# Moving x_lo by 128 bytes and the shared area by 256 in SBUF, in a one-core kernel of float32r matmuls

## What is computed

```python
proj = x @ w_in                                  # 2048 to 9552 columns
y = mem_cross_attention(x, mem, w_q_mem, w_kv_mem, w_o_mem)
g, u = jnp.split(x @ w_in, 2, axis=-1)           # the feed-forward layer
y = (jax.nn.silu(g) * u) @ w_out
```

## Time and profile before

| | before |
|---|---|
| time, median of 3 runs | 2236.54 us (2236.3 to 2237.06) |
| the profiled execution's span | 2233.7 us |
| TensorE matmul busy | 2221.8 us, 99% |
| TensorE weight load busy | 1840.4 us, 82% |
| VectorE busy | 1299.9 us, 58% |
| ScalarE busy | 1050.6 us, 47% |
| GpSimd busy | 179.5 us, 8% |
| read from HBM | 417.98 MB, 188 GB/s |

### The profile page before, as it was taken

How to read it: one execution, slowest core, us unless ns; L and a number is a source line. 1 busy time by engine, 2 the same in 40 slices (tenths; PEclk the granted TensorE clock), 3 DMA queues, 4 the chain that set the end, 5 groups by cost and what they waited for, 6 DMA issues and landing times.

```text
span 2233.7 us, 29393 instructions
## 1 busy us (share of the span) xinstructions
PE 2221.8 (99%) x10217; PEld 1840.4 (82%) x10217; DVE 1299.9 (58%) x1569; ACT 1050.6 (47%) x1263; POOL 179.5 (8%) x187
## 2 busy tenths in 40 slices
PE   9999999999999999999999999999999999999999
PEld 8888888888888888888888888888888888888887
DVE  5555655666667754454445445566656656645674
ACT  4444445555444644433444344446445444545643
POOL 1000000001304220000000000003000000200020
PEclk9999999999999999999999999999999999999999
DMA  7755654556856466656665566554566655665554
GB/s 234 227 171 163 195 158 144 190 171 216 256 180 214 134 198 190 206 199 194 188 191 187 197 190 187 191 205 151 170 188 194 207 179 183 211 189 174 169 189 165
DMA packets 216871, 421.30 MB, mean 189 GB/s; under 512 B 15400, under 2 KB 19536, under 8 KB 215120
## 3 DMA queue, kind: packets, MB, share of 16 engines
q1 hardware_dynamic: 212928, 401.79, 57.0%
q0 software_dynamic: 3584, 17.83, 2.4%
q10 hardware_dynamic: 272, 0.52, 0.1%
HBM read 417.98 MB, written 2.11 MB: 188 GB/s over the span
## 4 chain that ended last, share of the span: by engine, by line
PE 96%; DVE 2%; POOL 1%; DMA 1%; ACT 1%; issue 0%; ACTq 0%; DVEq 0%; SPq 0%; POOLq 0%
PE b_ps L665 90%; PE b_ps L707 1%; PE b_ps L812 1%; DVE b_w_lo L1667 1%; PE b_ps L724 1%; DMA b_stage<-in_w_in 1%; PE b_ps L827 1%; POOL b_x_res L549 0%; PE b_ps L821 0%; POOL b_x_res L551 0%; PE b_ps L903 0%; PE b_ps L880 0%; PE b_ps L828 0%; ACT b_w_hi L1209 0%; DVE b_x_res L1828 0%
## 5 line engine op out<-in xcount | busy, mean ns | idle before, releaser
L1667 DVE TENSOR_TENSOR b_w_lo<-b_stage,b_w_hi 128x1024 fp32r<-128x1024 f32 (+1 forms) x756 | 933.1, 1253 | 607.7 <-ACT b_w_hi L1209 604.2
L1209 ACT ACTIVATE b_w_hi<-b_stage 128x1024 fp32r<-128x1024 f32 (+1 forms) x758 | 790.4, 1054 | 678.5 <-PE b_ps L665 644.5
L665 PE MATMUL b_ps<-b_w_hi,b_x_hi 128*128 128x512 f32 (+1 forms) x2356 | 933.7, 396 | 2.2 <-DVE b_x_lo L1734 1.1
L665 PE MATMUL b_ps<-b_w_hi,b_x_lo 128*128 128x512 f32 (+1 forms) x2356 | 916.5, 389 | 0.0
L665 PE MATMUL b_ps<-b_w_lo,b_x_hi 128*128 128x512 f32 (+1 forms) x2356 | 915.0, 388 | 0.0
L665 PEld LDWEIGHTS b_ps<-b_w_hi,b_x_hi 128*128 128x128 f32 x2356 | 442.6, 188 | 93.0 <-issue 3.5
L665 PEld LDWEIGHTS b_ps<-b_w_hi,b_x_lo 128*128 128x128 f32 x2356 | 442.2, 188 | 92.9
L665 PEld LDWEIGHTS b_ps<-b_w_lo,b_x_hi 128*128 128x128 f32 x2356 | 442.9, 188 | 87.3
L665 PE MATMUL b_ps<-b_w_hi,b_ff_h 128*128 128x512 f32 x344 | 134.2, 390 | 0.0
L665 PE MATMUL b_ps<-b_w_hi,b_ff_l 128*128 128x512 f32 x344 | 133.9, 389 | 0.0
L665 PE MATMUL b_ps<-b_w_lo,b_ff_h 128*128 128x512 f32 x344 | 133.8, 389 | 0.0
(11 more groups left out here) (328 smaller groups left out, 1504.9 us busy)
## 6 DMA issues: line engine op xcount, KB each, us to landing
b_stage<-in_w_in SPq DMA_DIRECT2D x333, 512.0 KB, 4.2
b_stage<-in_w_ffn_in SPq DMA_DIRECT2D x176, 512.0 KB, 4.5
b_stage<-in_w_ffn_out SPq DMA_DIRECT2D x86, 512.0 KB, 4.1
b_stage<-in_w_out SPq DMA_DIRECT2D x64, 512.0 KB, 4.1
b_stage<-in_w_up SPq DMA_DIRECT2D x24, 512.0 KB, 4.1
b_stage<-in_w_o_dsa SPq DMA_DIRECT2D x16, 512.0 KB, 4.5
b_stage<-in_w_o_moba SPq DMA_DIRECT2D x16, 512.0 KB, 4.3
b_stage<-in_w_kv_mem SPq DMA_DIRECT2D x16, 512.0 KB, 3.5
```

The source lines that it names most:

```text
L665: ins = mm(ps[:, ACC + r, 0:n], x[:, kt + t, rows], w(slot)[:, t, 0:n], start=first and t == 0 and k == 0, stop=last and t == GK - 1 and k ...
L1209: act.activation(upper(slot)[:, :, 0:n], landing(slot)[:, :, 0:n], ACT.Copy)\
L1667: dve.tensor_tensor(rest(slot)[:, :, 0:n], landing(slot)[:, :, 0:n], upper(slot)[:, :, 0:n].bitcast(F32), ALU.subtract).then_inc(sem("lo_d ...
```

## The change

Two pads grow. `between` is a new tile of 32 float32 (128 bytes in each partition) that nothing reads or writes, given out between x_hi and x_lo; `align`, another unused tile ahead of the shared area, grows by 128 bytes. All from x_lo to v_st and the small tiles move by 128 bytes, all of the shared area by 256.

```diff
@@ -176,6 +176,7 @@
         w_hi = sb("w_hi", [P, SLOTS, GK, NB], F32R)
         w_lo = sb("w_lo", [P, SLOTS, GK, NB], F32R)
         x_hi = sb("x_hi", [P, KT, S], F32R)
+        sb("between", [P, 32])
         x_lo = sb("x_lo", [P, KT, S], F32R)
         vec_a = sb("vec_a", [P, D])
         vec_b = sb("vec_b", [P, D])
@@ -213,7 +214,7 @@
         shift = sb("shift", [P, 8])
         ln_gc = sb("ln_gc", [P, 2, 4])
         ln_bc = sb("ln_bc", [P, 2, 4])
-        sb("align", [P, 112 - 3 * 8])
+        sb("align", [P, 112 - 3 * 8 + 32])
 
 
         def shared(*shapes):
```

## The result

The changed kernel takes 2261.68 us (median of 4 runs, 2261.34 to 2261.98), the one before beside it 2236.42 (median of 4, 2234.94 to 2237.06): a ratio of 1.011, interval 1.0095 to 1.0124. The profiled span grew from 2233.7 to 2260.0 us, by 26.3. The forecast was no change.

The account below looks back on a forecast made before the run. TensorE was taken to bound the kernel: number of matmuls times the distance between starts. All terms of the change were 0, so 2233.7 us of span plus 2.8 us for the timed runs' median gave 2236.5 us; range 2213 to 2264.

Parts of the forecast that it names:

- 4408 pairs: Large matmuls whose operands' places change: 2368 with x_lo as stationary operand and 2040 with a shared pair.
- the 1.0 ns on each: Smallest tellable change, 4.5 us or about 0.2%, spread over the 4408 large matmuls whose places change.
- Between them I take 0: Price of the 4408 changed matmuls, set at 0 between a gain of 49.8 us and a loss of 59.5 us.
- would hide more: Caveat on lines 903 and 812: their matmuls stream 256 columns in 215 ns, half the large ones' pace.
- 8.3 ns of surplus: Line 1101's 256-column float32r matmuls, 115 ns each against 106.7; share of place or smaller weight left open.
- Rival A: Stationary and moving operands at different places modulo 512 slow each of 4408 matmuls: 2245, 2264 or 2296 us; chance 0.25.
- point of decision: Unequal places count as costing from 1 ns on for each of the 4408 changed matmuls.
- its 2264: Time if only the shared area's 2040 matmuls, 256 bytes apart, pay 13.5 ns more each, 27.5 us.
- If x_hi's matmuls change as well: Sign that the place of the weight load running beside them counts, and that the wrong pairs were counted.
- Rival B: Equal places make both reads collide, costing 13.5 ns a matmul; moving apart gives 2213, 2210 or 2187 us; chance 0.20.
- the 13.5 ns of surplus: Time every large float32r matmul takes beyond streaming its columns, wide or narrow; 123 us over 9144 matmuls.
- the stated range: Forecast range for the changed kernel's time, from 2213 on the low side to 2264 on the high side.

Follow-up runs that it names:

- the last kernel: w_lo and x_lo both put at 256 modulo 512, w_hi, x_hi and the shared pairs at 128, against the kernel before the change: 2271.06 us, ratio 1.0154.

## Why the prediction was wrong

The bound was read rightly: TensorE at full clock, its distance from start to start the only thing that addresses could touch, and nothing else moved by more than 1 us (VectorE, ScalarE and the waits). 4408 pairs were counted as changed, and the 1.0 ns on each that separates no change from a change was the right yardstick.

The step that failed is the value taken for the float32r pairs: "Between them I take 0, by the two pairs of rows that compare equal with unequal places". Those rows are of float32 matmuls, which stream 256 columns in 215 ns. They are as indifferent in the kernel after (0.86, 1.31 and 1.73 us again, and 0.66 us at line 813 with 128 bytes between its tiles) while the large ones pay: 25.3 us in place of 0, all of it with x_lo's move, 10.7 ns for each matmul of x_lo. The text had said that they "would hide more", and still let them decide; the row nearest in kind, line 1101's float32r with unequal places and 8.3 ns of surplus, had been set aside as open. It rose by 1.6 ns now that x_hi and x_lo lie apart.

Rival A, at a chance of 0.25, had the condition: a stationary operand that doesn't begin where the moving one does. That the two reads get in each other's way, its reason, no run shows. Its point of decision held (10.7 ns against 1 ns), and its modulus (512, where the runs have 256) and its placing didn't: it gave its 2264 to the shared area, 256 bytes apart, "with a second surplus of 13.5 ns on the shared area alone (2040 matmuls, 256 bytes apart)". The shared area costs 0, since 256 bytes count as none; the 25 us come from x_lo. It was also priced per changed matmul, while of the 13 ns in a clean stretch 5.7 fall on the x_hi matmul before x_lo's and 7.3 on x_lo's own. The prediction had named that case, "If x_hi's matmuls change as well": the pairs were then counted wrongly, and so they were, though the reason that it gave, the load beside them, missed by 28 us in the last kernel.

Rival B, that equal places cost the 13.5 ns of surplus, is wrong for the 512-column matmuls, which are nearly all of the time: at none of the seven unequal differences did a stretch of them run faster than at equal places, and with all tiles at 0 the surplus stays. Single distances do fall below that (224 ns comes back in every pattern of the kernel with w_lo and x_lo at 256), and longer ones beside them outweigh it. Only the 336-column matmuls gave 2.3 ns back, with w_lo alone displaced, 0.2 us in all. The 518 cycles, some 216 ns, that the Trainium skill gives for 512 columns ("TensorE: Matmul & The Clock Gate", Back-to-back issue gap) aren't reached at any of the places, where the shortest is 226.8 ns; what the surplus is made of, no run here shows. The same page's account of two independent read ports, by which loading the next weights takes nothing from the running matmul (Part 2, "Step-by-step: what each phase is for"), leaves no room for what these runs show: by the addresses alone a stretch of the same loads and matmuls runs at 226.8 ns a matmul or at 229 to 234. Whether the load is what delays the matmul, no run shows.

That the time lay inside the stated range is luck: its upper end was A's 2264, a cost put on the shared area, which costs nothing.

No version beats the kernel before: the best of the twelve tried are equal to it.

## What to carry to other kernels

Where a float32r kernel is bound by 512-column matmuls back to back, keep every large stationary and moving tile at one place modulo 256 bytes in the partition; which of the two tried, 0 or 128, made no difference, and unequal places cost 0.5 to 2.3% here without a single instruction changed. Check it in the chain of the profile: divide a clean piece of matmuls by its count, and compare the pieces of different tiles. The busy share (99 and 100%) doesn't show it, and a recorded duration (390 and 397 ns) is not the distance. And don't price an effect of the fastest stream by rows of a slower one, however equal they compare.

## What was not expected of the hardware

The step at 256 bytes and not at 512, for matmuls of 512 columns: 128 bytes apart cost 25 us, 256 bytes nothing (2261.94 against 2236.84 us). The cost doesn't add up: with one unequal load in three the spans make it 3.7 ns a matmul with x, with all three only 4.8 (2267.9 less 2233.7 us over 7104), and the change's own places with the products in another order cost 8 us more. And the same loop has more than one pace: with w_lo alone displaced it ran at 231.1 ns in one stretch and at 233.3 in another (44.37 and 44.80 us for 192), each in a pattern of its own that held until the next small matmuls, which no theory here explains. With 336 columns 128 bytes between w and the x pair cost nothing, and w_lo alone displaced made them 2.3 ns faster.
